# Two pairs of few-token experts in three 16-bit passes, their split work on ScalarE and VectorE, and four moved steps

## What is computed

```python
def moe_ffn(x, router_w, router_b, w_gate, w_up, w_down):
    Bsz, S_, D_ = x.shape
    T = Bsz * S_
    xt = x.reshape(T, D_)
    scores = jax.nn.sigmoid((xt @ router_w).astype(jnp.float32))
    biased = (scores + router_b.astype(jnp.float32)).reshape(T, N_GROUPS, EXPERTS_PER_GROUP)
    group_score = lax.top_k(biased, MOE_TOP_K)[0].sum(-1)
    best_group = jnp.argmax(group_score, axis=-1).astype(jnp.int32)
    in_group = jnp.take_along_axis(biased, best_group[:, None, None], axis=1)[:, 0]
    local = lax.top_k(in_group, MOE_TOP_K)[1]
    expert_idx = best_group[:, None] * EXPERTS_PER_GROUP + local
    gate = jnp.take_along_axis(scores, expert_idx, axis=1)
    gate = gate / gate.sum(-1, keepdims=True)
    n_assign = T * MOE_TOP_K
    flat_e = expert_idx.reshape(n_assign)
    order = jnp.argsort(flat_e)
    sorted_e = flat_e[order]
    sorted_tok = (order // MOE_TOP_K).astype(jnp.int32)
    sorted_w = gate.reshape(n_assign)[order]
    counts = jnp.zeros((N_EXPERTS,), jnp.int32).at[flat_e].add(1)
    padded = (counts + MOE_BLOCK - 1) // MOE_BLOCK * MOE_BLOCK
    pad_end = jnp.cumsum(padded)
    pad_start = pad_end - padded
    start = jnp.cumsum(counts) - counts
    dest = pad_start[sorted_e] + jnp.arange(n_assign) - start[sorted_e]
    n_blocks = -(-n_assign // MOE_BLOCK) + N_EXPERTS
    P = n_blocks * MOE_BLOCK
    buf_tok = jnp.full((P,), T, jnp.int32).at[dest].set(sorted_tok)
    buf_w = jnp.zeros((P,), x.dtype).at[dest].set(sorted_w.astype(x.dtype))
    block_expert = jnp.minimum(jnp.searchsorted(pad_end, jnp.arange(n_blocks) * MOE_BLOCK, side='right'), N_EXPERTS - 1)
    x_pad = jnp.concatenate([xt, jnp.zeros((1, D_), xt.dtype)], axis=0)
    xb = x_pad[buf_tok].reshape(n_blocks, MOE_BLOCK, D_)

    def expert_block(args):
        xi, e = args
        return (jax.nn.silu(xi @ w_gate[e]) * (xi @ w_up[e])) @ w_down[e]

    yb = lax.map(expert_block, (xb, block_expert)).reshape(P, D_) * buf_w[:, None]
    y = jnp.zeros((T + 1, D_), yb.dtype).at[buf_tok].add(yb)[:T]
    return y.reshape(Bsz, S_, D_)
```

## Time and profile before

| | |
|---|---|
| median of 3 runs | 1268.88 us (1268.79 to 1269.4) |
| time of the profiled execution | 1269.33 us |
| span that its profile shows | 1267.5 us |
| PE busy | 1231.5 us (97%) |
| DVE busy | 836.3 us (66%) |
| ACT busy | 623.5 us (49%) |
| share of the chain that ended last | PE 82%, DVE 9%, ACT 2%, DMA 1% |
| experts of layer 0 in the trace | about 770 to 954 us |
| experts of layer 1 in the trace | about 1076 to 1260 us |

### The profile page before, as it was taken

How to read it: one execution, slowest core, us unless ns; L and a number is a source line. 1 busy time by engine, 2 the same in 40 slices (tenths; PEclk the granted TensorE clock), 3 DMA queues, 4 the chain that set the end, 5 groups by cost and what they waited for, 6 DMA issues and landing times.

```text
span 1267.5 us, 17602 instructions
## 1 busy us (share of the span) xinstructions
PE 1231.5 (97%) x7091; PEld 672.3 (53%) x7091; DVE 836.3 (66%) x1066; ACT 623.5 (49%) x697; POOL 94.4 (7%) x60
## 2 busy tenths in 40 slices
PE   7999999999999999999999999999999999999997
PEld 4676555446664444555655765443444664554343
DVE  6678667878775468646557857633577786843475
ACT  4467475435554355535445743453455464444361
POOL 1000000000000003100002400002001400000200
PEclk9999999999999999999999999999999999999999
DMA  9475444546665673647664003779965720468990
GB/s 319 155 249 167 146 135 148 203 168 222 200 216 199 219 245 134 236 163 248 206 205 139 2 1 117 283 274 401 410 249 187 238 68 34 175 233 323 409 388 33
DMA packets 102765, 258.08 MB, mean 204 GB/s; under 512 B 7890, under 2 KB 15261, under 8 KB 102685
## 3 DMA queue, kind: packets, MB, share of 16 engines
q1 hardware_dynamic: 102684, 256.97, 57.2%
HBM read 255.87 MB, written 1.07 MB: 203 GB/s over the span
## 4 chain that ended last, share of the span: by engine, by line
PE 82%; DVE 9%; issue 3%; ACT 2%; DMA 1%; DVEq 1%; POOL 1%; POOLq 1%; SPq 0%; ACTq 0%
PE ps L1136 12%; PE ps L1415 8%; PE ps L1186 7%; PE ps L1142 6%; PE ps L841 6%; PE ps L1395 4%; PE ps L816 4%; PE ps L1462 4%; PE ps L1097 3%; PE ps L868 3%; PE ps L847 3%; PE ps L1444 2%; PE ps L822 2%; PE ps L1496 2%; PE ps L1524 2%
## 5 line engine op out<-in xcount | busy, mean ns | idle before, releaser
L2146 DVE SCALAR_TENSOR_TENSOR w_ring<-w_ring,w_hi 128x2048 f16<-128x2048 f32 (+3 forms) x155 | 348.2, 2257 | 114.2 <-ACT w_hi L1695 113.4
L1695 ACT ACTIVATE w_hi<-w_ring 128x2048 f16<-128x2048 f32 (+3 forms) x155 | 285.6, 1851 | 171.5 <-PE ps L1186 50.9
L1136 PE MATMUL ps<-actT,w_hi 128*128 128x512 f16 x608 | 137.5, 379 | 0.3 <-DVE arena L2140 0.3
L1695 ACT ACTIVATE arena<-ps 128x256 f16<-128x256 f32 (+8 forms) x97 | 66.2, 695 | 127.9 <-PE ps L1142 76.0
L1136 PEld LDWEIGHTS ps<-actT,w_hi 128*128 128x128 f16 x608 | 59.4, 98 | 64.6 <-DVE arena L2140 0.8
L816 PE MATMUL ps<-w_hi,actT 128*128 128x512 f16 (+2 forms) x384 | 82.2, 367 | 1.5 <-ACT w_hi L1695 1.5
L841 PE MATMUL ps<-w_hi,actT 128*128 128x512 f16 x352 | 83.2, 379 | 0.0
L1142 PE MATMUL ps<-actT,w_ring 128*128 128x256 f16 x608 | 72.6, 273 | 0.0
L1142 PEld LDWEIGHTS ps<-actT,w_ring 128*128 128x128 f16 x608 | 59.5, 98 | 15.0
L2031 ACT ACTIVATE arena<-ps 128x256 f32<-128x256 f32 x32 | 12.2, 383 | 110.8 <-PE ps L1415 73.9
L700 POOL TENSOR_TENSOR stats<-stats 128x1 f32<-128x1 f32 x14 | 17.6, 1254 | 578.6 <-DVE stats L2215 292.9
(11 more groups left out here) (460 smaller groups left out, 2108.8 us busy)
## 6 DMA issues: line engine op xcount, KB each, us to landing
w_ring<-in_dil_w_in SPq DMA_DIRECT2D x36, 1024.0 KB, 5.2
w_ring<-in_w_ff SPq DMA_DIRECT2D x32, 1024.0 KB, 5.1
w_ring<-in_w_in SPq DMA_DIRECT2D x24, 1024.0 KB, 5.0
w_ring<-in_exp_w_gate SPq DMA_DIRECT2D x48, 512.0 KB, 8.5
w_ring<-in_exp_w_up SPq DMA_DIRECT2D x48, 512.0 KB, 9.7
w_ring<-in_exp_w_down SPq DMA_DIRECT2D x20, 1024.0 KB, 13.9
w_ring<-in_sb_w_in SPq DMA_DIRECT2D x12, 1024.0 KB, 5.3
arena<-in_exp_w_down SPq DMA_DIRECT2D x10, 1024.0 KB, 13.1
```

Source lines behind the costliest of these rows:

```text
L1136: pe.matmul(ps[:, bank + c, :], w_h[:, k, c * P:(c + 1) * P], aT[:, kk, :], start=(kk == 0), stop=False, skip_group_check=True)
L1695: return act.activation(dst, src, ACT.Copy, scale=scale)
L2146: dve.scalar_tensor_tensor(out=lo16(h)[:, 0:kn * c], in0=slot(h)[:, 0:kn * c], scalar=W_POW, in1=hi16(h)[:, 0:kn * c], op0=ALU.mult, op1=A ...
```

## The change

1. The gate and up products of the pairs (8, 9) and (10, 11) are made of three 16-bit passes (`split_up`). Their 8 halves of each layer go through `hi` and `lo` (`split_half`), with new entries in the three SPLIT tables; their `silu` and gates are rescaled. Their down products and the other two pairs stay float32.
2. Fills 0 to 7: ScalarE copies 512 columns with gain and bias and then rounds the first 256 (the two pairs in question); VectorE copies the other 256 in float32 and writes the remainder of the first 256. Both engines take part in each of the eight.
3. VectorE makes the one-hots and gates of the single experts after fills 0 and 1 and one more `lo`.
4. Near the end of each layer's experts the first half of up(15) stands ahead of the tokens of unit 12 and of down(13) and down(14).
5. The last `sb_r` uses banks 0 and 1 and no longer waits for `sb_rest(6)`.
6. The DMAs of the parameter rows are issued by ScalarE's queue, which then preloads its function table; VectorE waits for the transposed parameters and scales them before it touches x.

```diff
--- before.py
+++ after.py
@@ -74,12 +74,12 @@
-SPLIT_EARLY = {2: 1, 3: 1, 7: 2, 12: 1, 14: 1}
-SPLIT_LATE = {2: 1, 4: 1, 9: 2, 11: 2, 12: 1, 13: 2, 14: 1}
-SPLIT_LAST = {9: 1, 11: 1, 13: 1}
+SPLIT_EARLY = {2: 1, 3: 1, 4: 1, 5: 1, 6: 1, 7: 2, 12: 1, 14: 1}
+SPLIT_LATE = {2: 1, 4: 1, 5: 1, 6: 2, 9: 2, 11: 2, 12: 1, 13: 2, 14: 1}
+SPLIT_LAST = {6: 2, 9: 1, 11: 1, 13: 1}
...
-ROUTE_DVE = {"best": 1, "ids": 2, "pairs": 3, "rows": 4, "slots": 5, "gates": 6}
+ROUTE_DVE = {"best": 1, "ids": 2, "pairs": 3, "rows": 4, "slots": 7, "gates": 8}
@@ -89,24 +89,34 @@
-    return f % 2 == 0 if f < 8 else f != FILL_GATES
+    return f != FILL_GATES
...
-    return f >= 8 or f % 2 == 1
+    return f >= 0
...
-FILL_DVE = [6 + sum(dve_fills(x) for x in FILL_ORDER[:n]) for n in FILL_AT]
+FILL_DVE = [(4 if n < 3 else 6) + sum(dve_fills(x) for x in FILL_ORDER[:n]) for n in FILL_AT]
...
+
+
+def split_up(i):
+
+    return UNITS[i][0] in ((8, 9), (10, 11))
+
+
+def split_half(key):
+
+    return not raw(key[1]) or (key[0] == "up" and key[1] < 12)
...
 def is_pair(i):
@@ -155,7 +165,7 @@
-    RELEASES += _down + _up if _i == NU - 1 else _up + _down
+    RELEASES += _up[:1] + _down + _up[1:] if _i == NU - 1 else _up + _down
...
 def half_shapes(n):
@@ -201,10 +211,10 @@
-    SPLIT_NO.append((SPLIT_NO[-1] if SPLIT_NO else 0) + (not _late or not raw(_key[1])))
+    SPLIT_NO.append((SPLIT_NO[-1] if SPLIT_NO else 0) + (not _late or split_half(_key)))
...
-    if not _late or not raw(_key[1]):
+    if not _late or split_half(_key):
@@ -478,7 +488,8 @@
-        xg_f = arena[:, 16384:20480].rearrange("p (k s) -> p k s", k=KD)
+        xp_hi, xp_lo = (half(arena[:, o:o + 1024]).rearrange("p (k s) -> p k s", k=KD) for o in (16384, 17408))
+        xg_f = arena[:, 18432:20480].rearrange("p (k s) -> p k s", k=KD)
@@ -537,8 +548,6 @@
-            sp.dma_start(prow[0:NPROW, 0:P], a["p_rows"][0:NPROW, :]).then_inc(sig("ld_params"), 16)
-            sp.dma_start(prow[0:NCOL - NPROW, P:2 * P], a["p_rows"][NPROW:NCOL, :]).then_inc(sig("ld_params"), 16)
@@ -1386,7 +1395,24 @@
-                        c = 128 * (block_of(i) - 4)
+                        c = 128 * ((block_of(i) - 4) % 2)
+                        if split_up(i):
+                            for b in range(2):
+                                hs = [2 * n0 + EXPERT_AT["up", r, b] for r in ranks]
+                                w = [rounded(h) for h in hs]
+                                for m, x in enumerate((xp_hi, xp_lo, xp_hi)):
+                                    if m == 2:
+                                        for h in hs:
+                                            rest_of(h)
+                                    for k in range(4):
+                                        kk = 4 * b + k
+                                        for j in range(2):
+                                            ins = pe.matmul(ps[64 * j:64 * j + 64, bank, :], x[:, kk, c + 64 * j:c + 64 * j + 64],
+                                                            gate_and_up(w[j][m // 2], k), start=(kk + m == 0),
+                                                            stop=(kk == KD - 1 and m == 2), skip_group_check=True)
+                                            if m == 2 and k == 3:
+                                                ins.then_inc(sig("w_used"), 1)
+                            return
@@ -1593,10 +1619,10 @@
+                up(NU - 1, (0,))
...
-                up(NU - 1, (0,))
@@ -1624,12 +1650,13 @@
-                if m:
+                bank = 0 if m == H2 // 2 - 1 else 4
+                if m and bank:
...
-                    pe.matmul(ps[:, 4 + j, 0:384], low, sb_l[m][:, j, :], start=True, stop=False,
+                    pe.matmul(ps[:, bank + j, 0:384], low, sb_l[m][:, j, :], start=True, stop=False,
...
-                    ins = pe.matmul(ps[:, 4 + j, P:S], ones, sb_l[m][:, j, S:384], start=False, stop=True,
+                    ins = pe.matmul(ps[:, bank + j, P:S], ones, sb_l[m][:, j, S:384], start=False, stop=True,
@@ -1734,6 +1761,9 @@
+            act.dma_start(prow[0:NPROW, 0:P], a["p_rows"][0:NPROW, :]).then_inc(sig("ld_params"), 16)
+            act.dma_start(prow[0:NCOL - NPROW, P:2 * P], a["p_rows"][NPROW:NCOL, :]).then_inc(sig("ld_params"), 16)
+            act.preload_act_table_set("exp_and_others")
@@ -1999,7 +2029,7 @@
             def experts(layer, n0, turn):
-                halves = [h for h in range(2 * n0, 2 * n0 + 3 * NE) if not raw(expert_key(h)[1])]
+                halves = [h for h in range(2 * n0, 2 * n0 + 3 * NE) if split_half(expert_key(h))]
@@ -2029,7 +2059,7 @@
-                                   scale=1.0 if is_pair(i) else 1.0 / SUM_POW).then_inc(sig("moe_silu"), 1)
+                                   scale=1.0 if is_pair(i) and not split_up(i) else 1.0 / SUM_POW).then_inc(sig("moe_silu"), 1)
@@ -2048,7 +2078,9 @@
                         if f < 8:
-                            ins = copy(xg_f[:, f, :], src, *gain(f))
+                            copy(x_rows[:, f % 2, :], src, *gain(f))
+                            act.drain()
+                            ins = copy(xp_hi[:, f, :], x_rows[:, f % 2, 0:S], A_POW)
@@ -2219,6 +2251,14 @@
+            dve.wait_ge(sig("params_T"), 1)
+            dve.tensor_copy(pcol[:, :], ps[:, 0, 0:NCOL])
+            dve.drain()
+            for name, n in (("ssd_norm", 4), ("g_mlp", 24), ("g_mix", 17)):
+                c = pcol[:, PROW[name]:PROW[name] + n]
+                ins = dve.tensor_scalar(c, c, A_POW, None, ALU.mult)
+            ins.then_inc(sig("pcol"), 1)
+            dve.drain()
@@ -2229,14 +2269,6 @@
-            dve.wait_ge(sig("params_T"), 1)
-            dve.tensor_copy(pcol[:, :], ps[:, 0, 0:NCOL])
-            dve.drain()
-            for name, n in (("ssd_norm", 4), ("g_mlp", 24), ("g_mix", 17)):
-                c = pcol[:, PROW[name]:PROW[name] + n]
-                ins = dve.tensor_scalar(c, c, A_POW, None, ALU.mult)
-            ins.then_inc(sig("pcol"), 1)
-            dve.drain()
@@ -3016,15 +3048,20 @@
                         if f < 8:
-                            ins = scaled(xg_f[:, f, :], src, *gain(f))
+                            dve.wait_ge(sig("route_act"), ACT_STEPS * layer + FILL_ACT[f])
+                            dve.tensor_copy(xg_f[:, f, :], x_rows[:, f % 2, S:2 * S])
+                            ins = dve.scalar_tensor_tensor(out=xp_lo[:, f, :], in0=x_rows[:, f % 2, 0:S], scalar=A_POW,
+                                                           in1=xp_hi[:, f, :], op0=ALU.mult, op1=ALU.subtract)
...
-                            dve.tensor_scalar(r_few[0:64, 4:8], ps[0:64, 6, 52:95:14], A_POW, None, ALU.mult)
-                            ins = dve.tensor_scalar(r_few[64:P, 4:8], ps[64:P, 6, 53:96:14], A_POW, None, ALU.mult)
+                            for j in range(2):
+                                r = slice(64 * j, 64 * j + 64)
+                                dve.tensor_scalar(r_few[r, 4:6], ps[r, 6, 52 + j:67 + j:14], A_POW / SUM_POW, None, ALU.mult)
+                                ins = dve.tensor_scalar(r_few[r, 6:8], ps[r, 6, 80 + j:95 + j:14], A_POW, None, ALU.mult)
@@ -3043,10 +3080,10 @@
+                fills((0, 1))
+                splits(1)
...
-                fills((0, 1))
-                splits(1)
@@ -3131,7 +3168,8 @@
-                dve.tensor_tensor(sb_z[m], sb_z[m], ps[:, 4:6, 0:384], ALU.subtract).then_inc(sig("sb_d"), 1)
+                bank = 0 if m == H2 // 2 - 1 else 4
+                dve.tensor_tensor(sb_z[m], sb_z[m], ps[:, bank:bank + 2, 0:384], ALU.subtract).then_inc(sig("sb_d"), 1)
...
```

## The result

The changed kernel takes 1282.99 us (median of 4 runs, 1281.33 to 1284.52) against 1269.04 (4 runs): the ratio is 1.0111, with a 95% interval of 1.0098 to 1.0123, so 14.0 us slower. The forecast was slower too, but by 6.3, and 1282.99 lies above its range.

What follows compares the result with a forecast made beforehand. PE, busy 97% of the span, was taken as the bound. Layer 0 +2.3, layer 1 +3.1, stick-breaking -0.3 and opening +1.2 sum to +6.3: median 1275.2 us from 1268.88; 8-in-10 range 1267.5 to 1282.

Steps and rivals of the forecast that it cites:

- The product: Pair products of units 6 and 7: 24 steps of 16-bit passes, 5.37 us instead of 7.02, 1.65 less each.
- the bound from the float32 products: Weight loads in the split product: a 0.11 us step carries two loads of 64 columns, so two fit 0.216.
- ACT's and DVE's queues: Experts, iterations 2 to 4 and 6 to 7: new work makes up(4) 1.3 us later and unit 7 4.6 later.
- What is given back: Vanishing PE waits: 0.8 us at 887.84 in layer 0, and 1.1 near the end of each layer.
- the stick-breaking: Last sb_r no longer waits 0.34 us for sb_rest(6): -0.3, between -0.34 and 0.
- The opening: Start of kernel: x waits for the parameter rows, +0.9 to +2.3 us, taken as +1.2.
- The other value that the forecast names for the term, 2.3: Opening: if another issuing engine saves only issue time, rows land nearer 7.9 than 6.5 and the term is 2.3 us.
- The bound of 6.7 us from issue to landing: Opening: parameter rows again take 6.7 us from issue, about 1.2 on ACT's queue, landing at 7.9; adds 1.4.
- (a): Rival, experts: faster because ScalarE's queue is no bound; -7.9 us, 1261.0; chance 0.09.
- (c): Rival, split products: array halves don't run side by side in 16 bits; +14 over the forecast, 1289; chance 0.04.
- (d): Rival, split products: weight loads stand between the steps, 0.49 us each; +18 over the forecast, 1293; chance 0.03.
- (b): Rival, experts and opening: ACT's and DVE's new work overlaps more, opening 0.9 or less; +2 or so, 1271; chance 0.14.

Runs made afterwards that it cites:

- no_split: Kernel before with parts 4 and 5 alone: no split of pairs, no new fills, old opening; 1266.12 us, ratio 0.9981.
- opening_queue: Kernel before with part 6 alone, but VectorE keeps its old order (x first, parameters after it); 1268.36 us, ratio 1.0.
- layers_only: Changed kernel with the old opening (parts 1 to 5 alone); 1277.83 us, ratio 1.0075 against the kernel before.
- kept_busy: Changed kernel with the old opening, plus products of zeros on PE ahead of unit 7's four waits; 1276.05 us, ratio 1.0058.
- rows_after_preload: Kernel before with part 6, VectorE's old order, and the table preload placed ahead of the rows' two DMAs on ACT's queue; 1270.15 us (one run).

## Why the prediction was right or wrong

**The product: right.** 5.30 for 24 steps against 5.37. Two weight loads of 64 columns fit a step of 0.22, as the bound from the float32 products said. The page "TensorE: Matmul & The Clock Gate" of the Trainium skill (part 3, "The mechanism") says in its list that a weight load overlaps running matmuls only when the row group differs, which would have the loads stand between the steps; the traces of all runs with the split speak against it.

**ACT's and DVE's queues: right in layer 0.** The fourth high part came 14.3 us after unit 6's end (14.2), up(4) came 1.41 later (1.3; in layer 1 it was 2.03, since less of a wait was there to give back), unit 7 ended 18.0 after unit 6 without a fall of the clock (17.9). Where I took the cause from one queue, moving the entry in that queue removed the wait at the fourth high part, but of up(4)'s it removed only 0.8 of 2.12: what remains above the 0.52 of before is the fill and not the half. The one term taken without a row, VectorE's copy of 256 columns at 0.17, measured 0.21 (811.07 to 811.28).

**What is given back, and the stick-breaking: right, and a little too small.** In `no_split`, 2.9 came against 1.1 + 1.1 + 0.3 = 2.5 of the forecast's terms.

**The opening: the step that failed first.** The forecast let the rows land between the identity (6.09) and 7.9, and wrote that the weights, 2.2 us earlier on SP, change nothing because ACT did not wait for the first. They landed at 10.65, and the identity, taken as unmoved, at 8.47. The other value that the forecast names for the term, 2.3, is too small as well. The mistake is to carry a landing time over from a row when the queue around it changes: what was asked is not who waits for the weights but what shares the DMA engines with the rows. The bound of 6.7 us from issue to landing was taken as an upper one; with x (1 MB), the identity and the first 1.5 MB of weights in flight at once it was 9.3. How that divides is known only in part: 1.15 went away with the weights 1.5 us later. With DVE's new order the experts then started 5.1 us late, and the kernel took 4.8 more instead of 1.2: 3.6 of the excess. With the old order (`opening_queue`) the same late rows cost nothing.

**The clock: the step that was missing.** The forecast names several waits inside one product, the longest of 2.5 us or more, and does not ask what PE's clock does behind them; it puts that term at nothing without a word. It fell in both layers of the profiled execution and in one of two layers of `layers_only`; a fall costs 0.7 (layer 0, where half of the slow stretch lies in the wait that vanished) to 1.5 in unit 7 and 1.7 behind up(4). The excess of the experts, 8.9 against 5.1, is of that size, though which execution has which falls is known only for the profiled ones: in `layers_only`, layer 0 without a fall is +1.8 at its end (forecast 2.3), layer 1 with two falls +6.8 (3.1). What could have warned stands in the opening of the kernel before: the sixteen transposes at 9.80, behind a wait of 2.59, take 2.97 us up to the next group at 12.77, 0.19 each, where two of the same shape take 0.22 at 841.49. The window there, in the kernel before:

```profile
8.00:16.00 8.00, 5.80 (x28) 4.26 (x28) 3.29 (x10) 3.77 (x6) 0.31 (x1) 0.79 1.10 343
```

**The rivals.** None came: not (a), (c) or (d), and not (b), the smaller cost. The forecast's range ended at 1282.0 because it took the opening's own bounds and nothing for the clock; with 3.6 and some 3 more it would have held 1282.99. The sign does not rest on these two terms: layer 0 of `layers_only`, with neither, is slower by 1.8.

## What to carry to other kernels

Work moved from the bounding engine to two others pays only where their queues have room at that moment: the same split saved 1.7 us in unit 6 and cost 4.6 in unit 7 even without a fall of the clock, with ACT half idle over the span. Price a wait inside a run of products twice, once as idle time and once for the slow steps that may follow it, and if it can't be removed, try harmless products in it (1.8 us here). In an opening, ask of every moved DMA what else is then in flight, and don't put the engine that everything waits for behind the one that lands last.

## What was not expected of the hardware

- **The granted clock falls behind waits of PE of 2.1 to 2.5 us, in some executions and not in others.** The same wait of 2.54 in unit 7 was followed by 0.50 in layer 1 of `layers_only` and by 1.00 in its layer 0. The Trainium skill's page "TensorE: Matmul & The Clock Gate" (part 1) says that the clock is set by how busy the array was; `kept_busy` agrees, with full clock in unit 7 and 1.8 us less with 24 products more in each layer. Why the same wait has both outcomes, no run here shows.
- **The granted clock in the windows doesn't show every slow stretch.** In the opening of the changed kernel all windows from 8 to 24 us say 1.00, while two products at 8.47 take 1.03 us where 0.61 is usual, and the sixteen transposes at 16.12 take 0.22 each where 0.11 is usual. Durations are the surer sign; in unit 7 both agree.
- **A DMA on ACT's queue isn't held up by a table load ahead of it.** In the timeline of `rows_after_preload` the load runs from 0.75 to 2.03, and the DMA that stands behind it in the program is issued at 0.78.
- **Early rows delay what is issued after them.** With the 78 KB of rows ahead, PE got the identity 1.3 us later after the identity's own issue on the same queue, and 2.3 us later with two queues.
